# Splitting the first output projection and its two norms by token halves, with modulation sums on VectorE

## What is computed

```python
# first block, end of the mixer and feed-forward part
mixed = jnp.concatenate([rmsnorm(out_a, g_a), rmsnorm(out_b, g_b), rmsnorm(out_c, g_c)], axis=-1)
x = x + rmsnorm(mixed @ w_out[l], attn_post_norm[l])
h = rmsnorm(x, ffn_pre_norm[l])
u = causal_depthwise_conv(h @ w_up[l], conv_w[l], conv_b[l])
gate, up = jnp.split(u, 2, axis=-1)
y = (jax.nn.gelu(gate, approximate=True) * up) @ w_down[l]
x = x + rmsnorm(y, ffn_post_norm[l])
# second block, beginning
mod = jax.nn.silu(c) @ w_ada[l] + b_ada[l]
sh1, sc1, gt1, sh2, sc2, gt2 = [m[:, None, :] for m in jnp.split(mod, 6, axis=-1)]
mod_c = jax.nn.silu(c_ctx) @ w_ada[l] + b_ada[l]
hc = modulate(rmsnorm_2(ctx, g_mix[l]), csh1, csc1)
h = modulate(rmsnorm_2(x, g_mix[l]), sh1, sc1)
```

## Time and profile before

| | us |
|---|---|
| median of three runs | 2752.36 |
| lowest and highest | 2749.18, 2754.35 |
| the profiled execution | 2751.02 |
| its span in the trace | 2749.2 |

### The profile page before, as it was taken

How to read it: one execution, slowest core, us unless ns; L and a number is a source line. 1 busy time by engine, 2 the same in 40 slices (tenths; PEclk the granted TensorE clock), 3 DMA queues, 4 the chain that set the end, 5 groups by cost and what they waited for, 6 DMA issues and landing times.

```text
span 2749.2 us, 34676 instructions
## 1 busy us (share of the span) xinstructions
PE 2542.0 (92%) x11946; PEld 1989.2 (72%) x11946; DVE 1556.9 (57%) x2441; ACT 1149.0 (42%) x1673; POOL 671.6 (24%) x401
## 2 busy tenths in 40 slices
PE   5999899979699999989999889999997899999996
PEld 2986467767278878767778777788874488888885
DVE  4132796642633350264542445288517899999997
ACT  3021353342133332333333431144324488888886
POOL 1221100012334446434457322230120011111100
PEclk9999999989799999999999999999998799999998
DMA  6010000004412322222222220100013899999995
GB/s 266 31 42 5 31 1 1 0 16 165 141 61 92 106 83 92 86 77 92 92 89 94 94 75 31 46 16 0 14 55 148 345 374 397 397 396 397 397 396 210
DMA packets 84179, 374.59 MB, mean 136 GB/s; under 512 B 7724, under 2 KB 8924, under 8 KB 70240
## 3 DMA queue, kind: packets, MB, share of 16 engines
q1 hardware_dynamic: 79344, 356.06, 34.3%
q0 software_dynamic: 4752, 17.43, 2.3%
HBM read 352.40 MB, written 21.05 MB: 136 GB/s over the span
## 4 chain that ended last, share of the span: by engine, by line
PE 75%; issue 9%; DVE 8%; POOL 4%; ACT 3%; DMA 1%; ACTq 0%; SPq 0%; POOLq 0%; DVEq 0%
PE ps L841 10%; PE ps L843 10%; PE ps L842 10%; PE ps L1103 6%; PE ps L1105 6%; PE ps L1104 6%; PE ps L674 5%; POOL w_lo L2117 3%; PE ps L666 3%; PE ps L811 2%; PE ps L731 2%; PE ps L733 2%; PE ps L732 2%; PE ps L686 2%; PE ps L1013 1%
## 5 line engine op out<-in xcount | busy, mean ns | idle before, releaser
L2117 POOL TENSOR_TENSOR w_lo<-arena,w_hi 128x1024 fp32r<-128x1024 f32 x172 | 413.2, 2403 | 839.9 <-ACT w_hi L1306 839.8
L2004 DVE TENSOR_TENSOR e_lo<-arena,e_hi 128x1024 fp32r<-128x1024 f32 x384 | 453.1, 1221 | 37.8 <-ACT e_hi L1513 25.3
L1513 ACT ACTIVATE e_hi<-arena 128x1024 fp32r<-128x1024 f32 x384 | 403.7, 1061 | 104.6 <-PE ps L1105 104.6
L1306 ACT ACTIVATE w_hi<-arena 128x1024 fp32r<-128x1024 f32 x172 | 181.4, 1055 | 432.4 <-PE ps L843 432.4
L841 PE MATMUL ps<-h_hi,w_hi 128*128 128x512 f32 x848 | 338.2, 399 | 17.3 <-issue 11.3
L843 PE MATMUL ps<-h_hi,w_lo 128*128 128x512 f32 x848 | 333.4, 393 | 0.0
L842 PE MATMUL ps<-h_lo,w_hi 128*128 128x512 f32 x848 | 333.3, 393 | 0.0
L1103 PE MATMUL ps<-e_hi,x_hi 128*128 128x512 f32 x512 | 203.6, 398 | 4.0 <-DVE e_lo L2004 4.0
L841 PEld LDWEIGHTS ps<-h_hi,w_hi 128*128 128x128 f32 x848 | 161.1, 190 | 61.1 <-issue 24.5
L1809 DVE SCALAR_TENSOR_TENSOR arena<-ps,cols,arena 128x511 f32<-128x511 f32 x88 | 63.8, 746 | 247.3 <-ACT arena L1356 247.3
L1105 PE MATMUL ps<-e_lo,x_hi 128*128 128x512 f32 x512 | 200.7, 392 | 0.0
(11 more groups left out here) (315 smaller groups left out, 4804.8 us busy)
## 6 DMA issues: line engine op xcount, KB each, us to landing
arena<-in_w_up SPq DMA_DIRECT2D x108, 1024.0 KB, 8.7
arena<-in_w_down SPq DMA_DIRECT2D x86, 1024.0 KB, 8.7
arena<-in_w_gate SPq DMA_DIRECT2D x64, 1024.0 KB, 10.2
arena<-in_w_in SPq DMA_DIRECT2D x18, 1024.0 KB, 4.8
arena<-in_w_ada SPq DMA_DIRECT2D x12, 1024.0 KB, 12.8
arena<-in_w_ada SPq DMA_DIRECT2D x16, 768.0 KB, 4.6
arena<-in_w_out SPq DMA_DIRECT2D x8, 1024.0 KB, 4.9
routed_rows<-arena SPq DMA_DIRECT2D x8, 520.0 KB, 2.7
```

What stands on the lines that cost most here:

```text
L1306: act_e.activation(w_hi[:, q, :], slot[c][:, q * D:(q + 1) * D], ACT.Copy).then_inc(s_whi, 1)
L1513: act_e.activation(e_hi[:, (2 * sl + a) % RING, :], slot[sl][:, a * D:(a + 1) * D], ACT.Copy).then_inc(s_ehi, 1)
L2004: v.tensor_tensor(e_lo[:, r, :], slot[sl][:, a * D:(a + 1) * D], e_hi[:, r, :].bitcast(F32), ALU.subtract).then_inc(s_elo, 1)
L2117: gp.tensor_tensor(w_lo[:, q, :], slot[c][:, q * D:(q + 1) * D], w_hi[:, q, :].bitcast(F32), ALU.subtract).then_inc(s_wlo, 1)
```

## The change

- **Output projection.** The weights of `w_out` are streamed twice (8 items in place of 4). A first pass makes the 8 tiles of the low half, a second one those of the high half. `m_hi` and `m_lo` are laid out by halves; the branch of the high half goes to `yT`'s place.
- **Norms 3 and 4** now cover the low half alone and are made among the products of the second pass: mean(3) in the middle of its first product, spread(3) in the middle of its second, mean(4) in its sixth, spread(4) in its seventh. VectorE adds the branch to x itself; GpSimd's additions are gone. ScalarE makes `h_hi` (line 1367 of the changed kernel), VectorE `h_lo`. The high half's norms are new, as 5 and 6, among the up products of the low half; the former 5 to 10 are 7 to 12.
- **The order of halved norms** (both halves): the 16 operations on the branch are cut into two groups of 8, one ahead of the taps of g = 2 and one ahead of those of g = 3; mean(6 or 8) comes after g = 5 and spread after g = 7.
- **Modulation.** Blocks 2 to 4 are computed for c alone. VectorE multiplies 24 pieces of 128x1024 by a scalar for each partition and adds them up, during the low half's down products; they are loaded there too, three behind each of eight weight items. TensorE sums over the partitions by 24 products of 128x1 ahead of the high half's up. The high half's `split_input` waits for all 24.
- **After the high half's down.** The squares of ctx (norm 10) come behind those of the branch (norm 9), and TensorE waits for one evacuated bank of each kind, not for all that came before.
- x is loaded ahead of the third item of `w_out`, not behind the fourth.

```diff
-            with pe.Fori(0, 2) as m:
-                for c in range(2):
-                    for q in range(2):
...
-                            i.then_inc(tps, 1)
...
-            mean(3)
-            parts(0, range(2))
-            spread(3)
-            parts(0, range(2, KT))
-            mean(4)
...
+            for i in range(KT):
+                output_part(i)
+            output_part(KT, lambda: mean(3))
+            output_part(KT + 1, lambda: spread(3))
+            for i in range(2, 5):
+                output_part(KT + i)
+            output_part(KT + 5, lambda: mean(4))
+            output_part(KT + 6, lambda: spread(4))
+            output_part(KT + 7)
...
+                if half:
+                    pe.wait_ge(s_md, 3 * KT)
+                    for t in range(3 * KT):
+                        m = pe.matmul(ps[:, 4, t:t + 1], mod_sum[:, t * P:(t + 1) * P], con("mean")[:, 0:1], start=True, stop=True)
+                    m.then_inc(s_mod, 1)
                 up(half, 0, 0)
...
+                mean(5 + 2 * half)
                 up(half, 1, 1)
...
+                spread(5 + 2 * half)
+                for g in range(2, 6):
+                    up(half, g, g % 2)
+                mean(6 + 2 * half)
+                up(half, 6, 0)
+                up(half, 7, 1)
+                spread(6 + 2 * half)
```

The low half's up still waits for every copy out of the output projection (`pe.wait_ge(eva, T_DN + 4 * half)` stands ahead of `up(half, 0, 0)` as before), and it now waits for each tile of `h_lo` by itself. VectorE's part of the modulation is:

```diff
+                if half == 0:
+                    v.wait_ge(s_act, FT + 1)
+                    for i in range(3 * KT):
+                        w, total, weight = adaB[i % KT], mod_sum[:, i % 3 * D:(i % 3 + 1) * D], scT[:, i // 3, 0:1]
+                        v.wait_ge(s_al[i % KT], 16 * (FIRST_ADA[i % KT] + i // KT + 1))
+                        if i < 3:
+                            v.tensor_scalar(total, w, weight, None, ALU.mult).then_inc(s_md, 1)
+                        else:
+                            v.wait_ge(s_md, i - 2)
+                            v.scalar_tensor_tensor(total, w, weight, total, ALU.mult, ALU.add).then_inc(s_md, 1)
```

## The result

The changed kernel takes 2725.59 us (median of 4 runs, 2725.36 to 2726.22); the kernel before took 2750.98 beside it (4 runs, 2749.18 to 2754.35). The ratio is 0.9906 with a 95% interval of [0.9895, 0.9918]: 25 us faster, where 44 were forecast (2707, range 2684 to 2724). The direction held. The size did not, and the time lies just outside the range.

A forecast was written before the change was run, and what follows sets the result against it. The prediction took a chain of two norms, 83.9 us between the last output product and up, as the bound; -53.3 + 8.3 + 4.5 + 2 - 5 - 1 = -44.5 gave 2707 us, range 2684 to 2724.

The forecast's parts named there:

- Up's start, -53.3: Second output pass to the low half's first up product: up begins at 712.2 against 765.5, 53.3 us saved.
- The 24 products, +2: Ahead of the high half's up: 24 modulation products cost 2.9 us, less about 1 of slow restart, +2.
- Behind down, -1: Behind the high half's down: the 7.99 wait goes, but norms set the end; -1 us (-4 to +3).
- VectorE's final split starts at 1596 to 1598: Behind the high half's down: VectorE's last split starts there against 1597.32 before, counted from the same end of down.
- Low half's up, +8.3: Low half's up: slow restart, transposes, small products and norm work delaying weights add 8.3 us (3 to 14).
- High half's up, -5: High half's up: the new norm order lets g = 7 end some 5 us earlier (0 to 9).
- Down, +4.5: Low half's down: VectorE's modulation pieces delay GpSimd's parts, 0.56 us idle on 8 items, +4.5 (0 to 12.5).
- GpSimd pays for each piece: Rival, low half's down: 0.9 us for each of 24 pieces, 21 in place of 4.5, 2724 us; chance 6 in 100.
- Locks: Second output pass: each `w_lo` part on GpSimd costs VectorE 2.2 us, as the two exclude each other.
- locks cost nothing: Rival, second output pass: no lock cost, up begins at 694, 2676 us in all; chance 8 in 100.
- The second pass starves further: Rival, second output pass: two more products wait as the fourteenth does, 19 us more, 2727 us; chance 12 in 100.
- the forecast's own case: Whole kernel: all forecast terms together, 2707 us; chance 72 in 100.

The follow-up runs named there:

- e1: Changed kernel with VectorE's three flags (s_uv twice, s_act) ahead of sums(5), not behind it: 2718.94 us, ratio 0.9879 to the kernel before.
- e2: Changed kernel with the 24 modulation products ahead of TensorE's wait for ScalarE's four tile copies: 2718.58 us, ratio 0.9877 to the kernel before.
- d3: Changed kernel with 23 of the 24 modulation products ahead of the high half's up left out, so modulation is wrong: 2713.91 us, ratio 0.9860.
- e3: Changed kernel with squares, sums, means and spreads behind the high half's down back in the order of the kernel before: 2717.75 us, ratio 0.9872.
- e4: Changed kernel with the old order behind the high half's down, but ctx's sums behind VectorE's four tile copies: 2719.45 us, ratio 0.9884.
- d2: Changed kernel with VectorE's 24 modulation pieces cut to one column, so modulation is not computed; loads, waits and signals stay: 2719.27 us, ratio 0.9881.
- d1: Changed kernel with GpSimd's low weight parts of the second pass and first up part cut to one column: 2713.72 us, ratio 0.9850.
- e6: Changed kernel with ScalarE's weight copy for the fourteenth output product ahead of the norm 4 squares that held it: 2723.98 us, ratio 0.9900.
- c0: Changed kernel with flags ahead of sums(5), products ahead of the wait for ScalarE and the old order behind down: 2713.63 us, ratio 0.9859.
- f1: Changed kernel with each of the 21 accumulating modulation pieces of 128x1024 made as two of 128x512, nothing left out: 2722.55 us, ratio 0.9899.
- d4: Changed kernel with each of the last 21 modulation pieces made two multiplications reading one SBUF tensor, sums wrong: 2723.19 us, ratio 0.9899.

## Why the prediction was wrong in size, step by step

- **Up's start, -53.3.** The steps up to ScalarE's last copy held: waits of 1.75 and 1.20 for mean(3) and spread(3) (2.0 and 2.1 said), 0.93 and 6.80 for weights (1.3 and 7.3), locked operations of 1.8 to 2.7 us, the last copy's end at 711.63 (712.2). What failed is the sentence "Up begins at 712.2": I asked what up's data needs and not what else stands in VectorE's order ahead of its flag. The earlier trace rows already had the row, `<-DVE tiny L1796`, a flag: there it stood right behind the split. e1 shows 7 us of the 7.7.
- **The 24 products, +2.** "8 took 0.95" read eight records of the earlier trace rows as eight products; four products of 128x1 make eight records. 48 records are 5.7 us by that row and 9.1 at the lower clock behind an idle time. The step "less about 1 of the slow restart" failed as well: e2 and d3 show that up restarts slowly with them and without them. d3: 9 us.
- **Behind down, -1.** The named waits came as said (7 and 6.5, measured 6.71 and 5.72), and the last sums ended 1 us sooner than before. What failed is "VectorE's final split starts at 1596 to 1598": it came 4.2 us later than before, counted from down's end. The step from mean(11) to the split was taken as unchanged, but mean(11) now stands inside ctx's product, and VectorE's copy of that product, ahead of the diagonal, waits 6.30 us. e3 and e4, with the old order, have the split 4 to 7 us earlier than the changed kernel. The traces of the changed order scatter by 2.5 us in this stretch, so of the 6.5 us that were missed some 2 may be chance.
- **Low half's up, +8.3.** Mechanism right, size 5.8: the two waits for weights were 0.52 and 1.21, not 3.9. The second group of eight operations met one locked part (2.91 us at 762.29), not two. In the high half it met two (2.72 and 2.88), and the waits were 2.35 and 4.56.
- **High half's up, -5.** Measured -4.2: TensorE's idle times in the stage fell from 15.3 us to 11.0. That the size fits is partly luck. The forecast's own terms, 10.34, two halves and 1.3 before against 2.6, 3.5 and two restarts of 1.9, make 2.7 and not 5.
- **Down, +4.5.** Against the kernel before it is 4.0, as said. But d2 shows the sums' whole price as 7: it is 3 us shorter than even the kernel before by the same marks (129.0, 132.2). The trace of before shows where those 3 us lay: behind waits of 2.19 and 2.69 us, 16 matmuls took 0.6 us or more there, in d2 none, and TensorE was busy 2.7 us longer. As the changed kernel has seven such matmuls, one or two of the 7 us may be the same scatter. The rival "GpSimd pays for each piece" (21) falls.
- **Locks.** The earlier trace rows gave 2.2 us a part; in the second pass it was 1.1 to 2.0. The rival "locks cost nothing" falls by d1. "The second pass starves further" falls too: no second wait like the 6.80 came, and e6 shows that most of that one was hidden by the norm chain.
- **Chances.** All rivals were about contention and starvation, none about a flag behind new work or a longer stretch behind down. So 0.72 for the forecast's own case was too much, and the upper end of 2724, the time of the rival in which GpSimd pays for each piece, missed by 2 us. c0, which undoes what cost the time in the three steps that failed (flags behind the sums, products behind a pause, the new order behind down), still took 2713.6, not 2707: single prices from medians and traces add up only within a few us.

## What to carry to other kernels

When work is put into a queue, list every signal that stands behind it there, pure flags too, and who waits for each. An engine that is let start earlier gains nothing when another engine's chain sets the end: the wait moves to where the chain is read next. When a step of such a chain is moved into a product, look at which copy of that product stands ahead of the chain's next step. Where GpSimd and VectorE must run side by side, short VectorE instructions cost GpSimd less than long ones.

## What the runs showed of the hardware

- 48 matmul records of 128x1 without any pause ahead of them took 6.65 us, and the ten matmuls of 512 columns behind them ran at the lower level of 1.2 GHz (0.63 instead of 0.39 us). Such small matmuls count as busy and still let the clock fall, as the windows of e2 show (columns as in the earlier trace rows; clock 0.82, then 0.55):

```profile
1103.50:1110.00 6.50, 6.46 (x48) 6.46 (x49) 1.98 (x3) 5.89 (x10) 2.35 (x1) 0.82 0.29 73
1110.00:1115.00 5.00, 5.00 (x14) 3.95 (x15) 3.01 (x6) 1.94 (x4) 0.00 (x0) 0.55 0.27 115
```

- An idle time of 2.56 us (f1) was followed by one matmul of 0.50 and then ones of 0.40, one of 3.08 at the same place (changed kernel) by one of 0.50, four of 0.40 and then seven of 0.63. But the length of the idle time doesn't tell alone: one of 2.19 at the head of the low half's down was followed by nine matmuls of 0.63 in the kernel before and by none in the changed kernel.
- The same stretch of 530 matmuls took 126.5, 128.1 or 129.6 us at a granted clock of 1.00, 0.99 or 0.97: behind the same two waits 0, 8 or 14 matmuls took 0.6 us or more, about 0.2 us each beyond a fast one.
- A VectorE multiplication of 128x1024 with one SBUF tensor as input took 0.75 us alone and up to 2.9 beside GpSimd's part of 2.4 (d4). Operations of 128x512 with two inputs, 0.69 to 0.75 alone, took 1.8 to 2.9 when they met such a part.
